# Rounding and subtracting weight blocks in two parts of 1024 columns in a three-layer fp32r kernel

## What is computed

```python
x = x + hyena_mixer(rmsnorm(x, norm_mix), ...)          # w_in 1024 x 3072, short conv, long conv by FFT, w_out
x = x + swiglu(rmsnorm(x, norm_ffn), gate, up, down)    # 1024 -> 2816 -> 1024
x = rmsnorm(x, norm_final)
for layer in range(2):
    h = rms_norm(x, g_mix[layer])
    x = x + (even_mixer(h, ...) if layer == 0 else odd_mixer(h, ...))
    m = rms_norm(mem, g_mem[layer])                      # 256 memory rows
    x = x + memory_cross_attention(rms_norm(x, g_xa[layer]), m, w_q, w_kv, w_o, ...)
    x = x + swiglu_2(rms_norm(x, g_ffn[layer]), w_gate, w_up, w_down)
return x
```

## Time and profile before

| what | value |
|---|---|
| median of 3 executions | 2246.02 us |
| the profiled execution, its own time | 2249.48 us |
| its span, first to last instruction | 2247.6 us |
| mean granted TensorE clock | 0.939 |
| PE busy | 2095.9 us (93%) |
| DVE busy | 1241.5 us (55%) |
| POOL busy | 822.9 us (37%) |
| ACT busy | 635.8 us (28%) |
| HBM read | 180.50 MB, 81 GB/s over the span |

### The profile page before, as it was taken

One profiled execution on the slowest core, in us unless ns is written; L12 is line 12 of the kernel. 1 busy time (PEld: TensorE's weight loads), 2 busy tenths in 40 slices (PEclk: granted clock), 3 DMA queues, 4 the chain that ended last, 5 costly groups with the idle time before them and its releaser, 6 DMA issues. The chain is left out here.

```text
span 2247.6 us, 22778 instructions
## 1 busy us (share of the span) xinstructions
PE 2095.9 (93%) x8907; PEld 1664.8 (74%) x8907; DVE 1241.5 (55%) x1481; ACT 635.8 (28%) x762; POOL 822.9 (37%) x203
## 2 busy tenths in 40 slices
PE   6888976999999999999996899999999968999998
PEld 5666765788888877555785788888787857888887
DVE  7776788754443467444756644433577658344301
ACT  3544111223222222211233232222222332232221
POOL 3365231344444433400241344444433513444443
PEclk8999988999999999855998999999999979999999
DMA  4121101222222231200230222222222312322232
GB/s 151 60 89 58 45 34 71 94 93 94 93 91 99 91 109 57 94 1 0 69 119 19 94 93 93 93 93 97 96 94 95 113 56 67 101 93 93 89 103 71
DMA packets 167771, 183.61 MB, mean 82 GB/s; under 512 B 4575, under 2 KB 156627, under 8 KB 166932
## 3 DMA queue, kind: packets, MB, share of 16 engines
q1 hardware_dynamic: 164612, 176.42, 23.9%
q10 hardware_dynamic: 3088, 6.20, 0.8%
HBM read 180.50 MB, written 2.10 MB: 81 GB/s over the span
## 5 line engine op out<-in xcount | busy, mean ns | idle before, releaser
L1781 POOL TENSOR_TENSOR w_lo<-w_raw,w_hi 128x2048 fp32r<-128x2048 f32 x167 | 771.2, 4619 | 1337.1 <-ACT w_hi L1446 1337.1
L490 PE MATMUL acc<-a_hi,w_hi 128*128 128x512 f32 x1544 | 613.8, 398 | 33.5 <-POOL w_lo L1781 16.2
L491 PE MATMUL acc<-a_lo,w_hi 128*128 128x512 f32 x1544 | 606.1, 393 | 0.0
L492 PE MATMUL acc<-a_hi,w_lo 128*128 128x512 f32 x1544 | 605.9, 392 | 0.0
L1446 ACT ACTIVATE w_hi<-w_raw 128x2048 fp32r<-128x2048 f32 x167 | 319.8, 1915 | 581.7 <-PE acc L492 577.7
L490 PEld LDWEIGHTS acc<-a_hi,w_hi 128*128 128x128 f32 x1544 | 292.7, 190 | 112.1 <-POOL w_lo L1781 20.7
L491 PEld LDWEIGHTS acc<-a_lo,w_hi 128*128 128x128 f32 x1544 | 293.0, 190 | 62.7 <-issue 2.2
L492 PEld LDWEIGHTS acc<-a_hi,w_lo 128*128 128x128 f32 x1544 | 292.2, 189 | 62.7
L492 PE MATMUL acc<-h_hi,w_lo 128*128 128x512 f32 x528 | 205.4, 389 | 0.0
L490 PE MATMUL acc<-h_hi,w_hi 128*128 128x512 f32 x528 | 205.4, 389 | 0.0
L491 PE MATMUL acc<-h_lo,w_hi 128*128 128x512 f32 x528 | 205.4, 389 | 0.0
(11 more groups left out here) (362 smaller groups left out, 2690.2 us busy)
## 6 DMA issues: line engine op xcount, KB each, us to landing
w_raw<-in_w_gate SPq DMA_DIRECT2D x22, 1024.0 KB, 5.0
w_raw<-in_w_up SPq DMA_DIRECT2D x22, 1024.0 KB, 5.0
w_raw<-in_w_down SPq DMA_DIRECT2D x16, 896.0 KB, 4.6
w_raw<-in_hy_w_in SPq DMA_DIRECT2D x12, 1024.0 KB, 5.0
w_raw<-in_ffn_w_gate SPq DMA_DIRECT2D x11, 1024.0 KB, 5.1
w_raw<-in_ffn_w_up SPq DMA_DIRECT2D x11, 1024.0 KB, 5.1
w_raw<-in_e_w_in SPq DMA_DIRECT2D x10, 1024.0 KB, 4.9
w_raw<-in_xa_wkv SPq DMA_DIRECT2D x8, 1024.0 KB, 4.8
```

The source lines that it names most:

```text
L490: nc.tensor.matmul(o, l_hi, r_hi, start=start, stop=False)
L491: nc.tensor.matmul(o, l_hi, r_lo, start=False, stop=False)
L492: return nc.tensor.matmul(o, l_lo, r_hi, start=False, stop=stop)
L1781: nc.gpsimd.tensor_tensor(w_lo[s][:, :], w_raw[s][:, :], w_hi[s][:, :].bitcast(F32), ALU.subtract)\
```

## The change

A block is rounded and subtracted in two parts of 1024 columns. ACT gives two copies, each of which raises `w_hi_ready` by one; POOL waits for each by itself, subtracts it, and raises `w_lo_ready` by one. So a block now counts two on both. PE waits for the first part at a block's start and for the second (`second_half`) ahead of the first product that reads it: at k = 4 of the first output of a wide or down block (12 matmuls in), at k = 2 of the first tile of a token block (6 matmuls in). Blocks of which at most 1024 columns are used, and the tables of the transforms, wait for both parts at the start (`whole=True`). SP waits for both parts of the block before last. What is computed is the same.

```diff
+HALF_BLK = BLK // 2
+BLK_HALVES = (slice(0, HALF_BLK), slice(HALF_BLK, BLK))
...
-        def block_in(k, width):
+        def second_half():
 
             pe.wait_ge(w_lo_ready, lo_seen.next())
+
+        def block_in(k, width, whole=False):
+
+            pe.wait_ge(w_lo_ready, lo_seen.next(2 if whole else 1))
...
-            wh, wl = block_in(kt, rows * outs)
+            wh, wl = block_in(kt, rows * outs, whole=kt * rows * outs <= HALF_BLK)
...
+                    if o == 0 and k * rows * outs == HALF_BLK:
+                        second_half()
...
+                        if t == 0 and k == 2:
+                            second_half()
...
-                wh, wl = block_in(TT, 512)
+                wh, wl = block_in(TT, 512, whole=True)
...
-            wh, wl = block_in(4, T)
+            wh, wl = block_in(4, T, whole=True)
...
+                            if o == 0 and k - k0 == 4:
+                                second_half()
...
-            S.activation(w_hi[b % 2][:, :], w_raw[b % 2][:, :], ACT.Copy).then_inc(w_hi_ready, 1)
+            for half in BLK_HALVES:
+                S.activation(w_hi[b % 2][:, half], w_raw[b % 2][:, half], ACT.Copy).then_inc(w_hi_ready, 1)
...
-            pool.wait_ge(w_hi_ready, hi_seen.next())
-            nc.gpsimd.tensor_tensor(w_lo[s][:, :], w_raw[s][:, :], w_hi[s][:, :].bitcast(F32), ALU.subtract)\
-                .then_inc(w_lo_ready, 1)
+            for half in BLK_HALVES:
+                pool.wait_ge(w_hi_ready, hi_seen.next())
+                nc.gpsimd.tensor_tensor(w_lo[s][:, half], w_raw[s][:, half], w_hi[s][:, half].bitcast(F32), ALU.subtract)\
+                    .then_inc(w_lo_ready, 1)
...
-                sp.wait_ge(w_lo_ready, lo_seen.next())
+                sp.wait_ge(w_lo_ready, lo_seen.next(2))
```

More of the change, by code:

```diff
@@ L686, in swiglu @@
             wide_block(a_hi, a_lo)
-            with counted_loop(pe, FT // 2 - 1, {lo_seen: 2, acc_freed: 4}):
+            with counted_loop(pe, FT // 2 - 1, {lo_seen: 4, acc_freed: 4}):
                 for _ in range(2):
@@ L1814, in _ @@
         left = len(block_outs) - 16
-        with counted_loop(pool, left // 2, {hi_seen: 2}):
+        with counted_loop(pool, left // 2, {hi_seen: 4}):
             for s in range(2):
@@ L1850, in swiglu @@
             n = n_blocks[0]
-            with counted_loop(sp, FT // 2 - 1, {lo_seen: 2}) as i:
+            with counted_loop(sp, FT // 2 - 1, {lo_seen: 4}) as i:
                 for w in (gate, up):
```

## The result

| | before | after |
|---|---|---|
| median of four runs each | 2246.59 us | 2223.82 us |
| lowest and highest | 2243.27 to 2247.4 | 2219.78 to 2224.88 |
| the profiled execution, its span | 2249.48, 2247.6 | 2224.73, 2222.9 |
| PE busy, PE idle within the span | 2095.9, 151.7 | 2091.8, 131.1 |

The ratio of the medians is 0.989, with a 95% interval of 0.9878 to 0.9902: 22.8 us faster, where the forecast was 12.4 us. The time lies in the range; the gain is nearly twice what was summed up. Of the 24.7 us by which the span is shorter, 20.6 are idle time of PE (151.7 less 131.1) and 4.1 busy time (2095.9 less 2091.8, with the same 8907 matmuls).

What follows compares the result with a forecast made beforehand. Only some 150 us of idle PE could shrink, mostly waits for w_lo and for DVE held by POOL. Terms 5.0+2.6+1.6+3.2 = 12.4 us, taken from 2246.0, gave 2233.6 us; range 2222 to 2244 us.

Steps and rivals of the forecast that it cites:

- The rival that the port is not let go between the halves: DVE stands through both of POOL's halves; gain only 5.5 us, so 2240.5 us; chance 0.17.
- ACT's half: ACT's copy of 1024 columns takes 1.05 us; the second instruction adds some 0.1 us per block, hidden.
- PE's second wait: Two waits per block on PE instead of one: zero cost, upper bound 5 us over 167 blocks.
- Memory key blocks: In each cross attention PE's 1.29 us wait for w_lo goes: 2.6 us gained.
- L1069: DVE operation behind the forward transform, held by w_lo; 0.8 us gained in each half of the channels, 1.6 us.
- The price of a half: POOL's subtraction of 1024 columns: 2.4 us, 0.4 more where DVE slips in; bounds 2.3 and 3.3 us.
- the slower rival: A half costs POOL over 2.73 us, lengthening waits for held DVE; at worst 13.5 us slower, 2259.5 us; chance 0.07.
- Thirteen other places where PE waits for a DVE that POOL holds: Ends of residuals, c_lo, xp, yo_lo, tmp: 0.25 us each, 3.2 us; bounds 0.3 loss to 1.8 gain each.
- The place that was walked: End of the hyena residual: earlier POOL catches one more operation, one more gets through; 0.25 us gained.
- hyena input: Stage from 57 to 223 us: 1.0 us less in each of three rounds, 5.0 us in all; bounds 0 and 8.
- the rival of 6.8 us: Shorter PE waits avoid two low-clock stretches, in hyena and at a residual's end: 6.8 us more, about 2227 us; chance 0.15.

Runs made afterwards that it cites:

- the eight-column kernel: Changed kernel with POOL subtracting only 8 columns of each half after the first two blocks, so not computing the reference: 2141.43 us, ratio 0.9533.
- the two kernels without ACT's head start: Changed kernel with ACT rounding each block in one instruction: 2219.76 us; the same with PE also waiting for both halves at a block's start: 2231.58 us.
- quarters: Changed kernel with ACT, POOL and PE working in four parts of 512 columns instead of two of 1024: 2190.29 us, ratio 0.9743 against the kernel before.
- eighths: Changed kernel with eight parts of 256 columns per block instead of two of 1024: 2170.64 us, ratio 0.9659 against the kernel before.
- the two part-kernels: Changed kernel with halves only in the first 16 blocks, whole after: 2234.47 us; and whole in the first 16 blocks, halves after: 2224.5 us.

## Why the prediction was right and wrong

**Right: the mechanism.** DVE stands behind POOL's subtraction and gets one operation through between two POOL instructions. The rival that the port is not let go between the halves is refuted by L1037 above, which ends 0.54 us after the first half, while the second has 2.2 us to go. The Trainium skill, GPSIMD Engine Reference, Instruction dispatch, by which a POOL core takes up the next instruction with no barrier, had spoken for that rival; by the trace this does not keep DVE out. That the lengthening is a hold and not slow DVE work is what the eight-column kernel shows. The Trainium skill, SBUF — State Buffer, in its section on the two separate sides, calls the shared ports an exclusive lock for the whole of an instruction; this case agrees, at 2.74 us for L1038.

**Right: the small steps.** ACT's half 1.05 us, 2.01 for a pair where some 2.0 was forecast. PE's second wait: nothing. Memory key blocks: both waits of 1.29 us gone, 2.6 us as forecast. L1069, now L1081:

```profile
237.92 5.20 POOL L1795 TENSOR_TENSOR w_lo<-w_raw,w_hi 128x1024 fp32r<-128x1024 f32 x2 [21.31 <-ACT w_hi L1459]
...
238.96 1.91 DVE L1081 TENSOR_TENSOR mid<-mid,tmp 1x512 f32<-1x512 f32 x1
240.80 2.87 DVE L1082 TENSOR_TENSOR mid<-mid,tmp 1x512 f32<-1x512 f32 x1
```

L1081 ends 2.95 us after POOL begins and L1082 5.75 us after; the walk had 2.95 and 5.74. PE's two waits behind it fell from 3.73 to 2.89 us and from 3.74 to 2.88: 1.7 us, for 1.6. The price of a half, put at 2.4 us or 2.8 with DVE's slip, is 2.54 on the mean, below the 2.73 of the slower rival.

**The step that failed: "Thirteen other places where PE waits for a DVE that POOL holds", 0.25 us each, 3.2 us in all.** In the places of these kinds PE waits 7.2 us less (a_lo 2.25, xp 1.6, yo_lo 1.3, tmp 0.9, the three sums of squares 0.65, c_lo 0.5). The place that was walked went as walked, from a wait of 1.83 to one of 1.62 us. The timeline after:

```profile
426.58 5.22 POOL L1795 TENSOR_TENSOR w_lo<-w_raw,w_hi 128x1024 fp32r<-128x1024 f32 x2 [5.64 <-ACT w_hi L1459]
426.79 2.78 DVE L966 SCALAR_TENSOR_TENSOR a_lo<-x,param,a_hi 128x512 fp32r<-128x512 f32 x1
429.50 2.85 DVE L976 TENSOR_TENSOR sumsq<-sumsq,sq 128x512 f32<-128x512 f32 x1
```

Here the earlier POOL catches one operation more (L966), and that operation gives back what the other gained: in the two kernels without ACT's head start PE does not wait here at all. But it was not a typical place. At the end of each cross attention the timeline before reads

```profile
1244.24 0.69 DVE L970 TENSOR_TENSOR x<-x,acc 128x512 f32<-128x512 f32 x1
1244.79 4.50 POOL L1781 TENSOR_TENSOR w_lo<-w_raw,w_hi 128x2048 fp32r<-128x2048 f32 x1 [9.26 <-ACT w_hi L1446]
1244.96 4.61 DVE L953 TENSOR_SCALAR a_hi<-x,param 128x512 fp32r<-128x512 f32 x1
1249.60 0.75 DVE L954 SCALAR_TENSOR_TENSOR a_lo<-x,param,a_hi 128x512 fp32r<-128x512 f32 x1
1250.41 0.80 PE L490 MATMUL acc<-a_hi,w_hi 128*128 128x512 f32 x1 [5.85 <-DVE a_lo L954]
```

and the changed kernel's

```profile
1229.77 4.91 POOL L1795 TENSOR_TENSOR w_lo<-w_raw,w_hi 128x1024 fp32r<-128x1024 f32 x2 [8.41 <-ACT w_hi L1459]
1230.08 0.69 DVE L982 TENSOR_TENSOR x<-x,acc 128x512 f32<-128x512 f32 x1
1230.80 1.69 DVE L965 TENSOR_SCALAR a_hi<-x,param 128x512 fp32r<-128x512 f32 x1
1232.52 2.71 DVE L966 SCALAR_TENSOR_TENSOR a_lo<-x,param,a_hi 128x512 fp32r<-128x512 f32 x1
1235.29 0.79 PE L496 MATMUL acc<-a_hi,w_hi 128*128 128x512 f32 x1 [4.72 <-DVE a_lo L966]
```

POOL starts 0.31 us before L982, where before it started 0.55 us behind the same operation (L970); but L982 reads PSUM and is not held. So the earlier POOL catches nothing new. From the start of L970 or L982 to the end of a_lo it is 6.11 us before (1250.35 less 1244.24) and 5.15 after (1235.23 less 1230.08), and PE's wait falls from 5.85 to 4.72 us, in both cross attentions. In the kernel where POOL alone works in halves the stretch is 5.93 us, and PE still waits only 4.82: there the subtraction before this one, which held a sum of squares for 4.68 us before, delays DVE less, and DVE reaches L982 0.85 us earlier against PE's last matmul. So the cut alone brings 1.03 of the 1.13 us here, and ACT's head start 0.10. yo_lo fell from 3.89 to 2.55, tmp from 5.61 to 4.73; the xp waits of each cross attention from 15.71 to 14.84 and from 15.58 to 14.86. The places differ by what stands ahead of the held operation on DVE, and one of each kind had to be walked.

**Second: hyena input, 5.0 us forecast, 7.1 measured.** From round to round the lead of L1047 over the old L1035 (starts 102.72 and 99.84, for one) was 1.9, 2.9, 3.8 and 4.8 us: 1.0 for each of the three rounds with e_lo and o_lo, as forecast, and from 163.10 on it was 7.0. The other 2.2 are put down to the first-half start; in the kernel in which PE waits for whole blocks the stage ends at 217.63, 1.9 us later than in the changed one. What was left out is what comes before any taps, where the lead was 0.6, 1.2 and 1.8 us in the first three rounds. The first 0.6 of it came with no shorter wait: the matmuls behind 24.5 us ran at a mean granted clock of 0.65 before and at 1.00 after,

```profile
24.50:34.40 9.90, 9.89 (x27) 6.49 (x28) 9.56 (x10) 2.54 (x2) 4.53 (x1) 0.65 0.82 258
```

```profile
24.70:33.90 9.20, 9.16 (x28) 5.96 (x29) 7.71 (x14) 2.76 (x3) 4.99 (x2) 1.00 0.84 260
```

and the other kernels show this start either way, so it cannot be put down to the edit.

**Third: the clock.** The sum has no term for it, and PE's busy time is 4.2 us less (4.1 by the rounded figures of the page). That is the size of the rival of 6.8 us in part, which was given 0.15 beside the forecast; but of its two stretches the one in the hyena input did not come back: from 34 us to the stage's end PE is at the lower level for 18.5 us, for 17.3 before. Behind it the time is less nearly everywhere. PE's granted clock goes down behind its longer waits, and over the kernels above it is low for less time where waits are shorter; yet a busy time of 2088.5 us with the waits as before shows that 4.2 us in one pair of profiles is not proof that the edit brought them. That stays open.

The sum by the trace is 7.4 us of idle time up to the first s_hi matmul (the stage is 7.1 shorter, with 0.4 more busy time), 2.6 at the memory key blocks, 1.7 behind the transforms, 7.2 in the kinds named, 1.2 in three more waits for DVE that had no term (a tmp of the second half's transform, x and small), 0.4 behind PE's last matmul and 4.2 of busy time: 24.7 us. By its own terms the forecast had 5.0 + 2.6 + 1.6 + 3.2.

**Why halves recover only 23 of the 106 us.** With one long subtraction, the first held DVE operation takes up all of POOL's time, and the second follows free. With two halves, each holds one: of two held operations the second ends 5.56 us after POOL begins before (L954 above) and 5.46 after (L966). With shorter parts the second comes through long before POOL is done. In the stretch measured above, from L970 to the end of a_lo, quarters take 3.03 us and eighths 2.63; the same three operations undisturbed take 1.99. This was not seen when quarters were expected to do little better than halves. The eighths' timeline:

```profile
1190.78 7.24 POOL L1808 TENSOR_TENSOR w_lo<-w_raw,w_hi 128x256 fp32r<-128x256 f32 x8 [3.92 <-ACT w_hi L1472]
1192.28 0.69 DVE L995 TENSOR_TENSOR x<-x,acc 128x512 f32<-128x512 f32 x1
1193.01 0.77 DVE L978 TENSOR_SCALAR a_hi<-x,param 128x512 fp32r<-128x512 f32 x1
1193.81 1.10 DVE L979 SCALAR_TENSOR_TENSOR a_lo<-x,param,a_hi 128x512 fp32r<-128x512 f32 x1
1194.96 0.50 PE L509 MATMUL acc<-a_hi,w_hi 128*128 128x512 f32 x1 [0.84 <-DVE a_lo L979]
```

PE's wait is down to 0.84 us, although POOL is at work for 7.24 us.

## What to carry to other kernels

When one GpSimd instruction reads SBUF for some us, look on VectorE for operations that end just behind it: that hold can cost more than the result's lateness does (here hold and lateness together were 77.8 us of TensorE's idle time, of which TensorE waited 18.7 us for the result itself). Cut the instruction into pieces down to where its fixed cost shows (256 columns and 0.83 us here), and expect little of two pieces where two held operations stand in a row. When many waits are priced by one that was walked, walk one of each kind, by what stands ahead of the held operation on its queue.

## What was not expected

- **A stage that the edit does not touch changes its length with the kernel.** POOL does nothing in the attention of the even mixer. It takes 127.38 us before. Its windows in the changed kernel and in the one with halves behind the first 16 blocks only are

```profile
938.94:1066.36 127.42, 125.70 (x306) 65.77 (x305) 55.71 (x142) 19.77 (x64) 0.00 (x0) 0.59 0.03 9
```

```profile
943.88:1063.26 119.38, 118.18 (x305) 62.50 (x305) 55.70 (x142) 19.80 (x64) 0.00 (x0) 0.63 0.04 12
```

  DVE and ACT work as long, but the granted clock is 0.59 in one and 0.63 in the other, mostly at the lower level of 1.2 GHz in both, and the stage takes 8.0 us longer in the changed kernel. With the even mixer's other part, where POOL does subtract, the spread over these kernels is 16 us. The kernel with halves behind the first 16 blocks has 11.6 us less than before in this stretch, which is most of why the two part-kernels do not add up. What sets it was not tried and stays open.
- The kernel with POOL whole and ACT in halves has two groups of times, 2243.56 to 2246.81 and 2250.27 to 2252.59 us, in ten runs. The granted clock goes with them: 0.942 to 0.945 in the first, 0.938 or 0.939 in four of the five of the second (0.943 in the fifth). The single highest runs of the kernels with PE's waits whole (2234.90), ACT whole (2228.70) and POOL alone in halves (2239.44) have a lower clock than their other three, too. What makes the clock differ between runs of one kernel stays open.
- A 1x512 operation, on one partition, is held by POOL like one of 128 (L1082, 2.87 us).
